# Two transformer blocks on one core: the projections of block 1 and the start of block 2 in three rounded products instead of one full f32 product

## The reference, cut to what matters

```python
for layer in range(DEPTH):                      # DEPTH = 2
    proj = jnp.einsum('bsd,de->bse', h, w_in[layer])
    ...
    ya = _from_blocks(oa) * jax.nn.silu(ag)
    yb = _from_blocks(ob) * jax.nn.silu(bg)
    yc = _from_blocks(oc) * jax.nn.silu(cg)
    y = jnp.einsum('bse,ed->bsd', jnp.concatenate([ya, yb, yc], axis=-1), w_out[layer])
    h = _layernorm(DEEPNORM_ALPHA * h + y, ln_g[layer], ln_b[layer])
...
score = jnp.einsum('bths,bth->bts', jax.nn.relu(logits), iwb) * idx_scale
_, sel = lax.top_k(score, topk)
```

## Time and profile before

| | |
|---|---|
| Time, median of 3 runs | 2115.94 us (2115.22 to 2116.03) |
| Profiled execution, span of its instructions | 2112.8 us |
| Median less span (start and end around the instructions) | 3.1 us |
| PE busy | 1902.5 us, 90% |
| DVE busy | 1142.6 us, 54% |
| ACT busy | 667.5 us, 32% |
| Mean granted PE clock | 0.942 |

### The profile page before, as it was taken

How to read it: one execution, slowest core, us unless ns; L and a number is a source line. 1 busy time by engine, 2 the same in 40 slices (tenths; PEclk the granted TensorE clock), 3 DMA queues, 4 the chain that set the end, 5 groups by cost and what they waited for, 6 DMA issues and landing times.

```text
span 2112.8 us, 19184 instructions
## 1 busy us (share of the span) xinstructions
PE 1902.5 (90%) x6900; PEld 1142.6 (54%) x6900; DVE 1142.6 (54%) x2306; ACT 667.5 (32%) x1340; POOL 25.4 (1%) x50
## 2 busy tenths in 40 slices
PE   5999999889899998989998876868999979999997
PEld 2444444434434444445333453556777868888785
DVE  4376676731999888532862352464445444444412
ACT  1123235311132344112112232335455334434411
POOL 2000000000000000000000000000000000000000
PEclk9999999999999998999998978978999979999998
DMA  6121112021211110032302011002333313332220
GB/s 219 40 80 40 41 49 67 27 80 40 80 40 40 40 70 1 1 111 72 89 20 60 12 59 30 14 18 75 90 90 102 113 41 99 100 98 84 98 100 40
DMA packets 153006, 135.79 MB, mean 64 GB/s; under 512 B 12673, under 2 KB 126977, under 8 KB 152913
## 3 DMA queue, kind: packets, MB, share of 16 engines
q1 hardware_dynamic: 149504, 124.53, 19.4%
q0 software_dynamic: 3408, 10.04, 1.6%
HBM read 130.36 MB, written 4.19 MB: 64 GB/s over the span
## 4 chain that ended last, share of the span: by engine, by line
PE 74%; DVE 16%; ACT 6%; issue 3%; DMA 1%; SPq 0%; DVEq 0%; ACTq 0%
PE proj L1262 24%; PE proj L1242 21%; PE proj L1259 11%; DVE rel_bias L1881 3%; PE proj L1239 2%; PE attn_out L1415 2%; PE score L1435 2%; PE score L1372 2%; PE proj L1435 1%; PE attn_out L1435 1%; PE turned_probs L1401 1%; DVE E L1951 1%; PE proj L1268 1%; PE turned_probs L1435 1%; DVE index_and_shared L1874 1%
## 5 line engine op out<-in xcount | busy, mean ns | idle before, releaser
L1262 PE MATMUL proj<-hT,weights 128*128 128x512 f32 x1216 | 561.9, 614 | 20.5 <-DVE raw L2135 11.4
L1262 PEld LDWEIGHTS proj<-hT,weights 128*128 128x128 f32 x1216 | 232.1, 196 | 302.6 <-issue 278.3
L1881 DVE SCALAR_TENSOR_TENSOR rel_bias<-index_and_shared,bias_deltas,rel_bias 128x128 f32<-128x128 f32 (+3 forms) x480 | 232.7, 547 | 4.3
L1242 PE MATMUL proj<-hT_high,weights_high 128*128 128x512 f32 x544 | 218.6, 402 | 7.6 <-DVE hT_low L2160 6.0
L1242 PE MATMUL proj<-hT_high,weights_low 128*128 128x512 f32 x544 | 215.8, 397 | 0.0
L1242 PE MATMUL proj<-hT_low,weights_high 128*128 128x512 f32 x544 | 215.5, 396 | 0.0
L2151 DVE TENSOR_TENSOR weights_low<-weights,weights_high 128x1024 fp32r<-128x1024 f32 (+1 forms) x122 | 135.3, 1116 | 96.4 <-ACT weights_high L1705 96.4
L1259 PE MATMUL proj<-weights,hT 128*128 128x512 f32 (+1 forms) x384 | 151.7, 553 | 0.1
L1705 ACT ACTIVATE weights_high<-weights 128x1024 fp32r<-128x1024 f32 (+1 forms) x122 | 111.5, 961 | 74.3 <-DMA weights<-in_w_ffn_down 60.5
L1242 PEld LDWEIGHTS proj<-hT_high,weights_high 128*128 128x128 f32 x544 | 103.2, 190 | 41.5 <-issue 9.5
L1453 ACT ACTIVATE tg<-proj 128x512 f32<-128x512 f32 x66 | 39.5, 599 | 267.0 <-PE proj L1242 212.2
(11 more groups left out here) (388 smaller groups left out, 2567.3 us busy)
## 6 DMA issues: line engine op xcount, KB each, us to landing
weights<-in_w_in SPq DMA_DIRECT2D x15, 2048.0 KB, 8.5
weights<-in_w_in SPq DMA_DIRECT2D x38, 512.0 KB, 4.2
weights<-in_w_ffn_gate SPq DMA_DIRECT2D x22, 512.0 KB, 4.1
weights<-in_w_ffn_up SPq DMA_DIRECT2D x22, 512.0 KB, 5.3
weights<-in_w_ffn_down SPq DMA_DIRECT2D x11, 1024.0 KB, 4.9
weights<-in_w_in SPq DMA_DIRECT2D x9, 1024.0 KB, 5.8
weights<-in_w_out SPq DMA_DIRECT2D x4, 2048.0 KB, 10.7
weights<-in_w_out SPq DMA_DIRECT2D x4, 1024.0 KB, 5.1
```

The lines of the kernel that those rows point to most:

```text
L1242: mm = nc.tensor.matmul(ps[:, :], w_[:, k, c0:c0 + P], x_[:, k, :], start=first, stop=last)
L1262: mm = nc.tensor.matmul(ps[0:gr["M"], :], w[:, k, c0:c0 + gr["M"]], x[:, k, :], start=first, stop=last)
L1881: ins = nc.vector.scalar_tensor_tensor(o, mk, d, o, ALU.mult, ALU.add)
```

## The change

All projections of 8 chunks now go the way of the tail. That is 114 groups: 33 and 8 in each of the two layers, 20 in the first stage of block 2 and 12 in HGRN. The slots are replaced by rings: a "slab" is now 128 columns (one piece of 4 KB per partition, 512 KB) or, for a T group, 512 columns in four pieces of two chunks each (`wide`). In block 1 the loaded pieces go round six places (`RAW_RING`) and the rounded ones four (`HIGH_RING`); a wide slab takes four places of either. The low part overwrites the loaded piece. From the latents on the rings have four and two places, in the tail nine and nine. `place_splits` puts the split of a piece in the list of steps behind the group that frees its place in the ring of rounded pieces (or two groups behind the one that frees the loaded place). The turned activations are kept as `hT_high` and `hT_low` from the start, so a "to_hT" bank is now given back by DVE (line 1782) and not by ACT. Before the output projection the mixed `y` is split too (`split_x`, 8 chunks per layer). The output projection now takes half 0 for all four tiles and then half 1, in block 2 two halves in place of four quarters, with the layer norm of a tile behind its second half. "to_hT" of the last tile moves between the second and third T group of the next stage. In the first stage of block 2 the slab for `V` of HGRN ("hi") comes before the other projections.

```diff
-W_SLOTS = 3
+SLOT = 4 * (KD * (P + 8))
+POOL_SLOTS = 10
+PIECE = 4 * KD * P
+RAW_RING, HIGH_RING = [SLOT * i for i in range(6)], [SLOT * i for i in range(6, 10)]
+RAW_RING_2, HIGH_RING_2 = RAW_RING[0:4], [SLOT * 8, SLOT * 9]
...
+TAIL_RING = 9
...
-        for t in range(NT):
-            group("T", sv, c0=0, N=512, K=KD, tile=t, dst=("V", 0), layer=l)
+        wide_tiles(sv, (0, 1), dst=("V", 0), layer=l)
+        turn_rows(NT - 1, **(dict(layer=l - 1) if l else {}))
+        wide_tiles(sv, (2, 3), dst=("V", 0), layer=l)
...
+        for c in range(6):
+            steps.append(("split_x", ("y", c, 1)))
+        wo = slab("wo", wide=True, cols=512, layer=l, half=0)
...
+        flush()
+        for c in (6, 7):
+            steps.append(("split_x", ("y", c, 1)))
+        steps.extend(("group", g) for g in late)
+        wide_tiles(wo, (2, 3), dst=("resid", 0), src="y", layer=l)
+        wo = slab("wo", wide=True, cols=512, layer=l, half=1)
         for t in range(NT):
-            for half in range(2):
...
+            wide_tiles(wo, (t,), dst=("resid", 1), src="y", layer=l)
             steps.append(("ln", (l, t)))
...
+def place_splits(steps, groups, slabs, pieces):
...
+    for i, p in enumerate(pieces):
+        for ring in ("raw", "high"):
+            p["free_" + ring] = max((slabs[o["slab"]]["last"] for o in pieces[:i] if any(
+                meets(p[ring], o[r], p["size"], o["size"]) for r in ("raw", "high"))
+                if o["slab"] != p["slab"]), default=-1)
...
+        seq = max(p["free_high"], min(p["free_raw"] + 2, slabs[p["slab"]]["first"] - 2))
+        assert seq < slabs[p["slab"]]["first"]
+        k = max(at.get(seq, -1), start[p["after"]], before)
+        while steps[k + 1][0] not in ("group", "half", "down"):
+            k += 1
...
+                        if s_["split"]:
+                            wh, wl = slab_view(WR, gr["slab"], "high"), slab_view(WR, gr["slab"], "raw")
+                            terms = ((wh, xh[src]), (wh, xl[src]), (wl, xh[src]))
...
+                    p = pieces[arg]
+                    act.wait_ge(p["loaded"], p["landed"])
+                    consumed(act, p["free_high"])
+                    nc.scalar.activation(piece_view(WR, p, "high"), piece_view(W, p, "raw"), ACT.Copy).then_inc(w_high, 1)
...
+                    p = pieces[arg]
+                    dve.wait_ge(w_high, p["nth"])
+                    nc.vector.tensor_tensor(piece_view(WR, p, "raw"), piece_view(W, p, "raw"),
+                                            piece_view(WR, p, "high"), ALU.subtract).then_inc(w_low, 1)
```

More of the change, by code:

```diff
@@ L197, in group @@
         if slab is not None:
-            slabs[slab]["last"] = g
+            used(slab, g)
             if state["mid"] and kw.get("K") == KD:
@@ L422, in plan @@
                     steps.append(("norm", dict(tile=t - 1, nth=t - 1)))
+                if t >= 2:
+                    turn_rows(t - 2, layer=l, norm=t - 2)
             elif t:
-                for half in range(2):
-                    group("to_hT", tile=t - 1, half=half, layer=l)
-            if final_layer and t >= 2:
-                for half in range(2):
-                    group("to_hT", tile=t - 2, half=half, layer=l, norm=t - 2)
+                turn_rows(t - 1, layer=l)
         if final_layer:
@@ L430, in plan @@
             steps.append(("norm", dict(tile=NT - 1, nth=NT - 1)))
-        for t in ((NT - 2, NT - 1) if final_layer else (NT - 1,)):
-            for half in range(2):
-                group("to_hT", tile=t, half=half, layer=l, **(dict(norm=t) if final_layer else {}))
+            turn_rows(NT - 2, layer=l, norm=NT - 2)
     if not only_block1:
-        second(steps, groups, slabs, items, units, state, slab, group, weave, flush)
-    annotate(steps, groups, items, units)
-    return dict(steps=steps, groups=groups, slabs=slabs, items=items, units=units)
@@ L442, in second @@
+def second(steps, groups, slabs, items, units, state, slab, used, group, turn_rows, wide_tiles, weave, flush):
     l = DEPTH
@@ L444, in second @@
     steps.append(("angles", 0))
-    state["slots"] = [0, 1]
-    s_iq = slab("iq", K=KD, cols=512)
-    s_ak = slab("avak", K=KD, cols=392)
+    s_av = slab("avw", cols=136)
+    for t in range(NT):
+        if t == 2:
+            turn_rows(NT - 1, layer=DEPTH - 1, norm=NT - 1)
+        group("T", s_av, N=136, K=KD, tile=t, dst=("av", 0))
     for c in range(4):
-        group("F", s_iq, c0=128 * c, M=P, K=KD, dst=("qk", 4 + c), scale=1.0)
+        group("F", slab("iq", c0=128 * c), K=KD, dst=("qk", 4 + c), scale=1.0)
@@ L557, in hgrn_gate @@
     def hgrn_gate(h):
-        g = group("gate", hold["last_hgrn"] if h < 3 else hold["hgrn"], c0=256, M=P, K=KD, chunk=4 + h, layer=l,
-                  first=False, unit=None)
+        g = group("gate", slab("hgrn", c0=HG + 128 * h), K=KD, chunk=4 + h, layer=l, first=False, unit=None)
         steps.append(("gate2", g))
@@ L616, in second @@
     steps.append(("split_x", ("mix", 7, 1)))
-    wo = tail[24:28]
-    for quarter in range(4):
-        last = quarter == 3
+    for half in range(2):
+        wo = slab("wo2", wide=True, cols=512, half=half)
+        last = half == 1
         for t in range(NT + last):
             if t < NT:
-                group("T", wo[quarter], c0=0, N=256, K=KD, tile=t, dst=("resid2", quarter), src="mix", parts=True)
-                if t in (1, 2):
-                    split_weights()
+                wide_tiles(wo, (t,), dst=("resid2", half), src="mix")
             if last:
@@ L628, in second @@
                 if t:
-                    for hh in range(2):
-                        group("to_hT", tile=t - 1, half=hh, norm=NT + t - 1, parts=True)
+                    turn_rows(t - 1, norm=NT + t - 1)
     for c in range(KF):
-        sl = tail[28 + c]
-        g = group("ffgate", sl, c0=0, M=P, K=KD, ring=c % 2, parts=True)
-        split_weights()
-        group("ffup", sl, c0=128, M=P, K=KD, chunk=c, ring=c % 2, gate=g, parts=True)
-        split_weights()
+        g = group("ffgate", slab("ffg", at=128 * c), K=KD, ring=c % 2)
+        group("ffup", slab("ffu", at=128 * c), K=KD, chunk=c, ring=c % 2, gate=g)
         if 2 <= c < EARLY + 2:
@@ L645, in second @@
             steps.append(("split_x", ("act", c, 1)))
-        steps.append(("down", dict(i=i, slab=tail[28 + KF + i])))
-        split_weights(2)
+        two = [slab("down", K=1, cols=1024, at=2 * i + k) for k in range(2)]
+        for sl in two:
+            used(sl, len(groups) + i)
+        steps.append(("down", dict(i=i, slabs=two)))
     for t in range(NT):
```

549 lines of the change are left out of this document (259 added, 290 removed).

## The result

| | before | changed |
|---|---|---|
| median | 2115.58 us (2113.88 to 2116.03, 4 runs) | 2214.7 us (2210.48 to 2217.82, 4 runs) |
| ratio to before, 95% interval | | 1.0466 (1.045 to 1.0483) |
| span of the profiled execution | 2112.8 us | 2215.6 us |
| mean granted PE clock | 0.942 | 0.887 |

The account below looks back on a forecast made before the run. PE bounds the kernel (90% busy), DVE is second in the layers, its fixed order delaying splits. Stage terms 9 − 24 + 9 + 12 + 20 + 24 − 8 + 6 = +48 gave 2164 us; 8-in-10 range 2095 to 2225.

Parts of the forecast that it names:

- PE's saving: All 114 projection groups: 6.87 us in f32 becomes 5.60 in three products, 1.27 us each, 145 us at most.
- Heads and woven part of layer 0: Layer 0 up to its flush: rope heads +5.4 and woven part −24, together −18.6 us.
- layer 1: Layer 1 up to its flush: heads +3.5 and woven part +9, together +12.5 us.
- woven parts: Layers before the flush: DVE's busy time plus its waits for ACT set the time; −24 us layer 0, +9 layer 1.
- heads: Start of each layer: first groups wait for splits and DVE's order; +5.4 us in layer 0, +3.5 in layer 1.
- Rival B: Gaps keep the clock low longer, ACT waits for loads: +133, 2249 us, chance 0.15; sign: 0.50 over 5 us.
- rival A: Splits hide in DVE's idle time: faster, −38, 2078 us, chance 0.19; sign: PE's split waits under 50 us.
- Output projection of layer 0: After layer 0's flush: 6.5 us gap between halves, a cold group, and banks behind layer norms on DVE; +12 us.
- Start of block 2: Output projection of layer 1 and start of block 2: turned banks wait behind DVE's norms, splits and angles; +20 us.
- Indexer: First stage of block 2: splits stand behind each top-k on DVE, so PE waits; +24 us.
- HGRN: Latents to HGRN: twelve groups save 15.5 us, splits on ACT and DVE cost 7.5; −8 us.
- tail: Block 2's output projection in halves: five splits stand ahead of a turned bank on DVE; +6 us.

Follow-up runs that it names:

- e2: Changed kernel with five places in each of the loaded and rounded rings (block 1, first stage of block 2) instead of six and four; 2189.8 us, ratio 1.0341.
- e5: Changed kernel with all but the first of each tile's bias steps cut to 32 columns, order kept; 2153.8 us, ratio 1.0173.
- e6: Kernel before the change with all but the first of each tile's bias steps cut to 32 columns; 2092.6 us, ratio 0.9879.
- e4: Changed kernel with the split subtractions of the first stage of block 2 on POOL instead of DVE; 2182.0 us, ratio 1.0306.
- e7: Changed kernel with the split subtractions of block 1 and of the first stage of block 2 on POOL instead of DVE; 2210.0 us, ratio 1.0445.
- e11: Changed kernel with block 1 in f32, its output projections tile by tile, and first-stage block 2 subtractions on POOL; 2127.7 us, ratio 1.0058.

## Why the forecast had the right sign and half the size

**PE's saving.** Right at the full clock: groups of 24 matmuls took 5.47 to 5.70 us in the woven parts and the indexer. But 145 us were to come off PE's busy time and 102 did, with the mean granted clock down from 0.942 to 0.887. In the woven part of layer 1, 27 groups at 1.27 us each would have brought PE from 312.9 to 278.6 us; it was 293.4. I had charged the clock only to single groups behind a gap.

**Heads and woven part of layer 0: −18.6 forecast, +13.2 measured; layer 1: +12.5 and +37.0.** This is the step that failed, and it alone is 56 us too low, where the whole sum was 55 too low (the errors of the other terms cancel, which is luck). Most of it is in the woven parts: +2.6 and +28.2 where I had −24 and +9; the heads were +10.6 and +8.8 where I had +5.4 and +3.5. I had written the woven part as DVE's busy time plus DVE's waits for ACT. The busy time was right. But the idle time of DVE that can't be filled is more than its waits for ACT. 10 us of layer 1's 39 stood in no wait of the list (gaps of hundredths of a microsecond between instructions). The waits for scores, 27.8 and 6.9 us before, I had put at nothing without a reason; 15.8 and 5.6 stayed. And the change made waits longer, of which one could have been read from the order: `bf`, a group of one piece behind a wide slab that fills the ring. I had priced the handover of a ring only where the rope heads begin (2.7 us) and between the halves (6.5 us, right), and not at two other places of each layer: behind `bvcv`, and ahead of the first half of `wo`, where PE waited 13.2 and 13.4 us. e2 and e5 with e6 show place and load for `bf` and the items; for `wo` no run does. In the heads, the +3.5 for layer 1 does not come out of my own terms either: 5.4 without the late start's 3.4 is 2.0, and less again without the turn.

**The bounds.** Each of these terms came out inside its own bounds and near the upper one (woven parts: +2.6 of at most +5, +28.2 of at most +30). My range took the terms as missing by about 10 us each, as if one miss said nothing of the next; they missed to the same side, for one cause. Rival B's terms were nearer in the layers (heads +10, layer 0 0, layer 1 +30) and at block 2's start with the indexer (+60, measured +57.7). Half of its mechanism shows: its sign, a clock of 0.50 for more than 5 us behind a gap, came at the start of block 2 (985 to 1020 us). The other half doesn't: no stretch of the woven parts shows ACT waiting for loads. The sign of rival A did not come: PE waited 123 us for splits in all, not under 50.

**Output projection of layer 0.** Right to 2 us in each step (half 0 was complete after 15.3 us, 17 forecast; the rest to 1 us), the cold clock included.

**Start of block 2: +20, measured +25.8.** The chain over DVE was right (the third bank let PE go on at 1005.27, 90.3 us after the flush; 89.4 forecast). Mis-sized was one term: two groups of 136 columns, "6", took 10.5 us at a clock of 0.50.

**Indexer: +24, measured +31.9.** Right in its mechanism: e4 takes all of it away. The first top-k started 58 us into the stage (54), and from there to the end of the last group it was 130 us, as forecast. Of the 4 us of late start about 1 is the cold clock (the first six groups took 34.8 us, 33.6 at the tail's rate) and 2 are a rounding and a split for which PE stood ahead of 1054.21; the other 4 us are the sums of squares behind the last group, 12.7 us where I had 9.

**HGRN −8, measured −10.8; tail +6, measured −4.9.** The tail's sign was wrong by a term that I had not looked at. Its output projection, to which the +6 belongs, got 10.7 us longer (70.1 to 80.8; PE's waits there for a turned bank went from 11.2 to 22.8). The stretch ahead of it got 8.2 us shorter and the feed-forward network 7.3 (384.8 to 377.5); why is not shown.

## What to carry to other kernels

Work added to an engine's fixed order is paid at its places as well as by its sum: list each handover of a ring (what must be finished before, what stands ahead of it in the order, what waits behind) and price every one, a wide slab's two ends above all. Look at the idle time of the second engine before you fill it: in layer 1, where DVE was busy for 88%, 34 us of splits and parts left 34 of its 39 us of idle time standing. Terms that rest on one mechanism miss together, so their bounds add up. Take the cheaper product where the second engine is idle and leave the stages alone where it isn't; here that turned +4.7% into −0.5%.

## What the runs showed of the hardware

A POOL subtraction of two SBUF operands holds up some DVE instructions beside it: four bias steps took 4.35 us in place of 2.21 beside one of 2.76 us (e7), and 128 x 1024 norm steps 3.00 and 3.25 us (e11) in place of 0.75 and 1.22 (changed kernel); MAX8 was not held up (e4). The Trainium skill bears on this in "SBUF — State Buffer", section "Who interferes with whom": a DVE instruction with two SBUF inputs contends with a GpSimd instruction that reads SBUF, and one in a 2-port mode and a GpSimd instruction block each other for the whole instruction. By that rule, the trace agrees: the bias step reads two SBUF operands, and the 2.1 us that it lost fit into one subtraction.

PE's clock stayed at 0.50 for 23 us in which PE was busy for all but about one, with matmuls of 136 columns; I had taken a busy engine for a warm one. More generally the granted clock fell where PE's waits grew, 0.93 to 0.86 in the woven part of layer 1.
